# Four staging places with a semaphore each, in place of two, in the last part of a hybrid HGRN2/S5 block

## The reference, cut to what matters

```
u = RMSNorm(h)
[q | f | i | g_hg | u_s5 | z_s5 | gate_hg | gate_s5] = u @ W_in
o    = hgrn2(q, f, i), per-head RMSNorm, * silu(g_hg)
y_hg = o @ w_o_hg
ys   = gelu(s5_scan(u_s5))
a, b = split(ys @ w_glu + b_glu);  y_s5 = (a * sigmoid(b) * silu(z_s5)) @ w_o_s5
h   += (sigmoid(gate_hg) * y_hg + sigmoid(gate_s5) * y_s5) @ w_out
h   += (p @ w_ple) * sigmoid(RMSNorm(h) @ w_ple_gate)
out  = RMSNorm(h)
```

## Time and profile before

| | us |
|---|---|
| timed runs | 2375.15, 2375.37, 2377.81 (median 2375.37) |
| profiled execution, its own time | 2378.16 |
| its span, first to last instruction | 2376.6 |
| PE busy | 2272.8 (96%) |
| DVE busy | 1199.0 (50%) |
| ACT busy | 919.9 (39%) |
| POOL busy | 146.8 (6%) |

### The profile page before, as it was taken

How to read it: one execution, slowest core, us unless ns; L and a number is a source line. 1 busy time by engine, 2 the same in 40 slices (tenths; PEclk the granted TensorE clock), 3 DMA queues, 4 the chain that set the end, 5 groups by cost and what they waited for, 6 DMA issues and landing times. The chain is left out here.

```text
span 2376.6 us, 30201 instructions
## 1 busy us (share of the span) xinstructions
PE 2272.8 (96%) x10800; PEld 1836.9 (77%) x10800; DVE 1199.0 (50%) x2230; ACT 919.9 (39%) x1360; POOL 146.8 (6%) x254
## 2 busy tenths in 40 slices
PE   6899999999999997999999999969999999999997
PEld 2688888888888886888777777758887777778775
DVE  5443444343444434111656566546566566665655
ACT  6343444443444434111233333333443354354343
POOL 0000000000000000110111111110001000100100
PEclk8899999999999999999999999989999999999998
DMA  4110101010100100322222222265336435634622
GB/s 160 36 36 23 45 9 44 9 49 18 35 26 26 41 18 14 86 65 85 78 78 87 87 77 80 77 202 167 118 114 212 153 99 177 212 107 135 219 90 79
DMA packets 89267, 206.37 MB, mean 87 GB/s; under 512 B 20832, under 2 KB 30048, under 8 KB 89184
## 3 DMA queue, kind: packets, MB, share of 16 engines
q1 hardware_dynamic: 68432, 139.68, 18.7%
q0 software_dynamic: 20752, 65.57, 8.3%
HBM read 157.87 MB, written 46.14 MB: 86 GB/s over the span
## 5 line engine op out<-in xcount | busy, mean ns | idle before, releaser
L95 PE MATMUL s_ps<-u_hi,s_w_hi 128*128 128x512 f32 x768 | 305.4, 398 | 8.7 <-DVE s_w_lo L875 8.7
L96 PE MATMUL s_ps<-u_lo,s_w_hi 128*128 128x512 f32 x768 | 300.0, 391 | 0.0
L97 PE MATMUL s_ps<-u_hi,s_w_lo 128*128 128x512 f32 x768 | 299.5, 390 | 0.0
L95 PE MATMUL t_ps<-t_oa_hi,t_w_hi 128*128 128x512 f32 x512 | 205.1, 401 | 13.8 <-DVE t_oa_lo L1555 9.9
L96 PE MATMUL t_ps<-t_oa_lo,t_w_hi 128*128 128x512 f32 x512 | 203.0, 396 | 2.5 <-issue 2.5
L97 PE MATMUL t_ps<-t_oa_hi,t_w_lo 128*128 128x512 f32 x512 | 202.7, 396 | 0.0
L1446 DVE TENSOR_TENSOR t_w_lo<-c_raw,t_w_hi 128x1024 fp32r<-128x1024 f32 x136 | 166.5, 1224 | 63.4 <-ACT t_w_hi L1352 63.4
L95 PEld LDWEIGHTS s_ps<-u_hi,s_w_hi 128*128 128x128 f32 x768 | 144.4, 188 | 52.6 <-issue 14.5
L97 PEld LDWEIGHTS s_ps<-u_hi,s_w_lo 128*128 128x128 f32 x768 | 144.5, 188 | 31.1
L96 PEld LDWEIGHTS s_ps<-u_lo,s_w_hi 128*128 128x128 f32 x768 | 144.6, 188 | 28.5
L1352 ACT ACTIVATE t_w_hi<-c_raw 128x1024 fp32r<-128x1024 f32 x136 | 142.4, 1047 | 41.7 <-PE t_ps L97 13.2
(11 more groups left out here) (280 smaller groups left out, 4786.6 us busy)
## 6 DMA issues: line engine op xcount, KB each, us to landing
c_raw<-w_in_in SPq DMA_DIRECT2D x56, 512.0 KB, 3.7
gates_scratch<-s_stage POOLq DMA_DIRECT2D x64, 256.0 KB, 2.7
t_ein<-gates_scratch SPq DMA_DIRECT2D x64, 256.0 KB, 4.4
c_raw<-w_o_hg_in SPq DMA_DIRECT2D x32, 512.0 KB, 5.0
c_raw<-w_out_in SPq DMA_DIRECT2D x32, 512.0 KB, 3.5
c_raw<-w_ple_gate_in SPq DMA_DIRECT2D x32, 512.0 KB, 3.5
c_raw<-w_glu_in SPq DMA_DIRECT2D x16, 512.0 KB, 4.2
t_xa<-o_gated_scratch POOLq DMA_DIRECT2D x32, 256.0 KB, 4.3
```

The lines of the kernel that those rows point to most:

```text
L95: pe.matmul(out, w_hi, u_hi, start=first, stop=False)
L96: pe.matmul(out, w_hi, u_lo, start=False, stop=False)
L97: return pe.matmul(out, w_lo, u_hi, start=False, stop=last)
```

## The change

`xa` gets four places of its own semaphore each (`xa_in`), and the borrowed halves of `xn` are given up. In the prologue the place of block n is n % 4; in a body it is counted anew from p0, so p0, y2, o2, o6 use place 0, p1, y3, o3, o7 place 1, y0, o0, o4 place 2 and y1, o1, o5 place 3. A load waits until the last user of its place is split: from y2 on that is the block four back; for p0 and p1 it is o6 and o7 of the body before, for y0 and y1 it is o4 and o5 of the body before, which by POOL's order lie behind already. `LOADS` counts how often a place is loaded in a body (4, 4, 3, 3), for the value that ACT waits for.

```diff
-    BANKS = 6
+    BANKS, XS = 6, 4
-        xa = m.sb("xa", [P, 2, TT])
+        xa = m.sb("xa", [P, XS, TT])
-        xa_in = [m.pool_dma_sem(f"xa_in{i}") for i in range(2)]
+        xa_in = [m.pool_dma_sem(f"xa_in{i}") for i in range(XS)]
-        def x_buffer(body, what, k, half):
-
-            return (xn if not body and what == "y" and k >= 2 else xa)[:, half]
-                sp.dma_start((xa if k < 2 else xn)[:, k % 2], y_source(k, 0)).then_inc(first_xa_in[k], 16)
+                sp.dma_start(xa[:, k], y_source(k, 0)).then_inc(first_xa_in[k], 16)
+        LAST_USER = [max(n for n in range(len(XBODY)) if n % XS == s) for s in range(XS)]
+        LOADS = [len([n for n in range(len(XBODY)) if n % XS == s]) for s in range(XS)]
-            def load_xa(n, half, what, k, t):
-                pool.wait_ge(x_lo_done, n - 1)
+            def load_xa(splits, slot_, what, k, t):
+                pool.wait_ge(x_lo_done, splits)
-                pool.dma_start(xa[:, half], src).then_inc(xa_in[half], 16)
+                pool.dma_start(xa[:, slot_], src).then_inc(xa_in[slot_], 16)
...
-                        load_xa(t * len(XBODY) + (len(XPRO) + n), n % 2, what, k, t if what == "p" else t + 1)
+                        base = len(XPRO) if isinstance(t, int) and t == 0 else t * len(XBODY) + len(XPRO)
+                        if n >= XS:
+                            splits = base + (n - XS + 1)
+                        elif first:
+                            splits = len(XPRO) - XS + n + 1
+                        else:
+                            splits = base - len(XBODY) + (LAST_USER[n] + 1)
+                        load_xa(splits, n % XS, what, k, t if what == "p" else t + 1)
             for n, (what, k) in enumerate(XPRO):
                 if what == "o":
-                    load_xa(n, n % 2, what, k, 0)
+                    load_xa(n - XS + 1, n % XS, what, k, 0)
...
-                return at, at % 2, at // 2 - S5KT // 2 + 1
-            return t * len(XBODY) + at, at % 2, t * (len(XBODY) // 2) + (at // 2 - S5KT // 2 + 1)
+                return at, at % XS, at // XS
+            n = at - len(XPRO)
+            return t * len(XBODY) + at, n % XS, t * LOADS[n % XS] + (KT // XS + n // XS + 1)
```

More of the change, by code:

```diff
@@ L1380, in round_x @@
                     act.wait_ge(xa_in[half], loads * 16)
-                src, dst = x_buffer(body, what, k, half), dict(y=acts_y, o=acts_a, p=acts_p)[what][0][:, k]
+                src, dst = xa[:, half], dict(y=acts_y, o=acts_a, p=acts_p)[what][0][:, k]
                 if what == "y":
@@ L1550, in split_x @@
                 hi, lo = (x[:, k] for x in dict(y=acts_y, o=acts_a, p=acts_p)[what])
-                src, hi = x_buffer(body, what, k, half), hi.bitcast(F32)
+                src, hi = xa[:, half], hi.bitcast(F32)
                 if what == "y":
```

## The result

The changed kernel took 2357.42 us in the median of 5 runs (2353.71 to 2359.15), the kernel before, beside it, 2377.81 (2375.15 to 2385.66): a ratio of 0.9908, 95% interval 0.9888 to 0.9929. That is 20.4 us less, where 33.2 were predicted. Of the 15 us, 2.4 are the base: the prediction started from 2375.4 us, and the kernel before took 2377.81 beside the changed one. The gain itself is 12.8 us short. The direction was right, and about 0.6 of the gain came.

The account below looks back on a forecast made before the run. Mostly PE's three products bound the kernel, with `xa` loads about 4% of the last part's chain. Gains of 19.5 (o loads), 8.0 (prologue) and 5.7 us (`h`, y2) sum to 33.2, taking 2375.4 to 2342.2 us; range 2338 to 2355.

Parts of the forecast that it names:

- The o loads: os5 into ohg, tiles 1 to 3: o blocks load earlier and go off PE's path; gain 19.5 us.
- Tile 2, 4.5 predicted: ohg of tile 2: the excess of 5.0 us goes except 0.5 us; gain 4.5 us.
- The 0.5 us a tile for the ohg weights: Start of ohg, tiles 1 to 3: o6 and o7 in flight delay the first weights; bounds nothing and 2.1 us.
- The weights rival: ohg, three tiles: first weights 2.1 us late and the lower clock back, 12.6 us lost, time 2355; chance 0.15.
- The prologue: glu and os5 before tile 0: `h` and o6 come about 7 us earlier, waits and slowed products go; gain 8.0 us.
- The 3.90 us go: os5 of the prologue: PE's 3.90 us idle goes, and about 3.3 of 3.6 us of slowed products.
- The cover of 2 us: os5 of the prologue: o6 lands at 1588, ACT is next wanted at 1590.3 or a little sooner; about 2 us.
- an earlier `h` then delays the os5 weights: Prologue rival: earlier `h` delays the os5 weights as it delayed o6; 7 us more, time 2349; chance 0.05.
- h, y2 and the first out weights: ohg into out, tiles 1 and 2: `h` and y2 come 2.5 us sooner; gain 5.7 us, bounds 0 and 7.1.
- this costs PE 0.67 us. I keep 0.7 us in each tile.: Start of out, tiles 1 and 2: `h` ahead of the first weights, as in tile 3, costs PE 0.7 us each.
- The rival that y2 stays where it is: Tiles 1 and 2: the `h` load, not the stores, sets y2; 5.7 us more, time 2348; chance 0.12.
- The rule: DMA engines alternate between queues, so POOL's loads take up to half from SP's ohg weight load: 2.1 us rather than 0.5.

Follow-up runs that it names:

- no_loop: The changed kernel with tiles 1 and 2 written out in place of the hardware loop on every engine: 2347.92 us, ratio 0.9871 to before.
- after: The changed kernel (four places for `xa`) against the kernel before: 2357.42 us, ratio 0.9908.
- after_again: The changed kernel timed and profiled once more, nothing altered: 2358.79 us, ratio 0.9914 to the kernel before.
- h0_late: The changed kernel with `h` of tile 0 loaded in its body, behind y3, in place of the prologue: 2352.66 us, ratio 0.9890 to before.
- h0_after_o7: The changed kernel with `h` of tile 0 behind o7 in the prologue in place of o5: 2359.63 us, ratio 0.9921 to before.
- y_first: The changed kernel with y2 and y3 loaded ahead of the stores and of `h`: 2353.20 us, ratio 0.9886 to before.
- before_h0_mid: The kernel before, two places, with only `h` of tile 0 moved out of the prologue to ahead of y1 in its body: 2374.21 us, ratio 0.9972.

## Why the prediction was off

The prediction summed 19.5 + 8.0 + 5.7 = 33.2 us; in the profiled executions these places gave 20.7.

*The o loads, right in mechanism.* They went off PE's path in all three tiles, with issues where they were forecast. In all they gave 15.4 us for 19.5. Tile 3 gave 8.1 us for 7.6. Two sizes were off:
- Tile 2, 4.5 predicted. The excess of 5.0 us was read from the window alone. Of its 2.82 us of idle time, 2.47 were a pause with no visible wait, which staging cannot fill; no_loop ties the changed kernel's pause to the loop's jump back. It moved to the section's first product, out of the window, and the lower clock that follows it stayed. Counted with the 1.7 us in os5 and without the 1.34 us of the `w_out` wait, ohg of tile 2 gave 1.1 us. 3.4 us too much.
- The 0.5 us a tile for the ohg weights. Their loads took 5.9 and 8.5 us in place of 6.9 and 5.8, and in tile 1 PE paid 1.23 us at the o6 that ACT could not reach, and the slower products beside it: the term gave 6.2 us for 7.4. Nearer to the low bound than to 2.1, but too low. The weights rival (2.1 us and the low clock in all three tiles) did not come: ohg ran at a clock of 1.00 in tiles 1 and 3.

*The prologue, wrong: 4.6 us for 8.0.* The failed step is "The 3.90 us go, and of the 25.34 - 21.76 = 3.6 us of slowed products in os5 about 3.3." The cover of 2 us was worked out for o6, which was fine. The weights of os5 were not followed; with `h` earlier they stand behind it. The rival "an earlier `h` then delays the os5 weights", 0.05 in the prediction, is what happened, at 3.4 to 4.5 of its 7 us (after, after_again). Its share of the chances was too small: it is the mechanism that came. h0_late, both kernels of before with `h` moved, and h0_after_o7 show it. The two-place kernel already had that collision, with o6 and o7 as its visible victims: with `h` moved away, its os5 takes 24.01 us, and that of the four-place kernel 23.60. It was not a cost of the places.

*h, y2 and the first out weights, wrong: 0.6 us for 5.7.* Out fell by 4.0 us, but PE's new pauses for `w_out`, 2.02 and 1.34 us, stand at the end of ohg and are paid there. What was 1.4 us in the sum (0.7 a tile) measured 6.5: these 3.4 us and 3.1 us of excess left in out. The failed step is "this costs PE 0.67 us. I keep 0.7 us in each tile." The wait for the stores shrank as forecast (3.48 us), but `h` was no longer issued in the same moment as the first `w_out` (before: 0.07 us behind it, 3.5 us to landing) but 2.15 us ahead of it, and PE paid for it in both tiles, with slowed products after it (out of tile 1 at a clock of 0.96). The price was taken from tile 3, where it still holds (0.52 us), but there no y blocks are in flight beside the weights, which land in 9.9 us in place of 11.3 and 10.7; whether y2 and y3 make that difference was not tried. y2 came 15.6 us behind `h`, not 13.65, with y3 now beside it. The rival that y2 stays where it is did not come: ACT had y2 46.75 us after PE began ohg of tile 1, and before 53.40. y_first shows that 5.6 us of this can be had.

*The rule.* The Trainium skill, DMA: Bandwidth & Descriptors, section "Queues, rings and completion order", has the queues take turns. Between issue and landing of that `w_out` load, the queues of the changed kernel did this (packets, MB, share of 16 engines):

```profile
q0 software_dynamic: 666, 2.56, 77.8%
q1 hardware_dynamic: 228, 0.86, 20.7%
```

q1, SP's queue, got a quarter of the packets and bytes, not half, and these do not come evenly. The same view of the first 3.7 us after the issue (1829.84 to 1833.5) shows q0 alone:

```profile
q0 software_dynamic: 204, 0.84, 95.7%
```

From 1833.5 on q1 moved 228 of 690 packets, a third; 0.86 MB is more than one load, as the second `w_out` load went out at 1835.32. So two things made the 11.3 us: nothing of the load moved for 3.7 us, and then its queue got a third. In which of the 3.7 us the load was ready to take a turn, the trace does not show. The turns, if they are taken, are not equal shares of the stretch; the measurement decides. As a warning the rule was good. Where the prediction used it, on the first ohg weights, it said more than came: PE paid 1.23 us in tile 1 and not the 2.1 us in each tile.

## What to carry to other kernels

A buffer that is no longer short lets its queue run ahead, so follow every large transfer behind it to its new issue time and list each load that is issued before it lands (12 to 17 us here); in the prologue one 2048 KB load decided more than the number of places. Place such a load just behind the urgent small ones, or where nothing urgent follows: moving that one DMA alone was worth 6 us with either number of places, and with two places nothing where it was put so late that its own user waited. And before an excess is booked to a cause, look at what ended each idle stretch in it: 2.5 of 5.0 us here were idle time that no load had caused.

## What was not expected of the hardware

- A 512 KB weight load issued from 0.07 us ahead of to 0.42 us behind a 2048 KB load of the other queue lands in 3.4 to 3.7 us; 0.53 to 0.93 us behind it, in 7.0 to 11.0; from 2.0 to 6.4 us behind it, in the bodies of the tiles, it lands within 2 us of the large one.
- At the jump back of the hardware loop PE idles 2.15 (h0_late) to 3.94 us (before_h0_mid) without a wait that explains it, once or in two parts, and in nine of the eleven profiles with the loop the section behind it has a granted clock of 0.93 to 0.97. In the three profiles without the loop that pause is gone, and the clock there is 1.00.
